# Three edits in a float32 network kernel: the up-projection's moving operand joined to 512 columns, the router's choice taken from logits, and slot weights as one product of six columns

## The reference

```python
def conv_glu_ffn(x, w_up, conv_w, conv_b, w_down):
    h = x @ w_up
    g, u = h[..., :D_FF], h[..., D_FF:]
    g = causal_depthwise_conv(g, conv_w, width=3) + conv_b
    return (jax.nn.silu(g) * u) @ w_down
```

```python
g_prob = softmax(h @ w_rg + b_rg)                  # 4 groups
g_top, g_idx = top_k(g_prob, 1)
e_in = (h @ w_re + b_re)[chosen group]             # 8 experts
e_top, e_idx = top_k(softmax(e_in), 2)
wts = g_top * e_top / sum(e_top)
y = sum over the two experts: wts * ((silu(h @ w_g[e]) * (h @ w_u[e])) @ w_d[e])
x = x + y
x = x + (p @ w_ple) * sigmoid(rmsnorm(x) @ w_ple_gate)
out = rmsnorm(x)
```

## Time and profile before

| | |
|---|---|
| Median of 3 executions | 1065.79 us (1063.05 to 1066.69) |
| The profiled execution's own time | 1061.78 us |
| Its span in the profile | 1060.0 us |
| PE busy | 1014.4 us (96%), weight loads 781.1 |
| DVE busy | 630.1 us (59%) |
| ACT busy | 533.6 us (50%) |
| POOL busy | 86.5 us (8%) |
| Bytes moved | 224.62 MB, mean 212 GB/s |

### The profile page before, as it was taken

How to read it: one execution, slowest core, us unless ns; L and a number is a source line. 1 busy time by engine, 2 the same in 40 slices (tenths; PEclk the granted TensorE clock), 3 DMA queues, 4 the chain that set the end, 5 groups by cost and what they waited for, 6 DMA issues and landing times.

```text
span 1060.0 us, 15388 instructions
## 1 busy us (share of the span) xinstructions
PE 1014.4 (96%) x6023; PEld 781.1 (74%) x6023; DVE 630.1 (59%) x1242; ACT 533.6 (50%) x941; POOL 86.5 (8%) x98
## 2 busy tenths in 40 slices
PE   7999899999999999999999999997989999999977
PEld 6777599999888876799999888775655455545445
DVE  4778678888646576678888547668642121212156
ACT  6667565555436566665555447746522122112255
POOL 0100002112000211002112002100000000000000
PEclk9999999999999999999999999999999999999999
DMA  8824255664565533465654563155459999999931
GB/s 279 312 89 150 81 159 163 196 199 160 200 197 178 180 127 113 125 193 161 198 199 160 186 187 129 41 165 196 162 174 410 409 409 409 409 409 409 405 110 40
DMA packets 112672, 224.62 MB, mean 212 GB/s; under 512 B 10559, under 2 KB 65234, under 8 KB 112594
## 3 DMA queue, kind: packets, MB, share of 16 engines
q1 hardware_dynamic: 112434, 223.04, 60.0%
q10 hardware_dynamic: 160, 0.53, 0.1%
HBM read 222.50 MB, written 1.05 MB: 211 GB/s over the span
## 4 chain that ended last, share of the span: by engine, by line
PE 86%; DVE 8%; ACT 3%; issue 1%; SPq 1%; DMA 1%; DVEq 0%; ACTq 0%
PE ps L543 82%; PE ps L547 4%; DVE wl L1890 1%; DVE smb L1904 1%; SPq L2795 1%; DMA ring<-in_w_in_even_dram 1%; DVE xs L1890 1%; DVE pb L1895 0%; ACT hh L1354 0%; DVE smb L1890 0%; ACT wh L1357 0%; ACT xh L1357 0%; SPq L2792 0%; DVE hl L1900 0%; ACT xg L1354 0%
## 5 line engine op out<-in xcount | busy, mean ns | idle before, releaser
L1890 DVE TENSOR_TENSOR wl<-ring,wh 128x1024 fp32r<-128x1024 f32 (+3 forms) x212 | 278.4, 1322 | 132.3 <-ACT wh L1357 130.9
L1357 ACT ACTIVATE wh<-ring 128x1024 fp32r<-128x1024 f32 (+3 forms) x212 | 222.6, 1052 | 147.1 <-PE ps L543 142.7
L543 PE MATMUL ps<-hh,wh 128*128 128x256 f32 x768 | 218.9, 286 | 1.4 <-DVE sA L1890 1.0
L543 PE MATMUL ps<-hh,wl 128*128 128x256 f32 x768 | 216.8, 283 | 0.0
L543 PE MATMUL ps<-hl,wh 128*128 128x256 f32 x768 | 215.1, 283 | 0.0
L543 PEld LDWEIGHTS ps<-hh,wh 128*128 128x128 f32 x768 | 147.6, 192 | 3.2 <-DVE wl L1890 1.4
L543 PEld LDWEIGHTS ps<-hh,wl 128*128 128x128 f32 x768 | 147.5, 192 | 0.0
L543 PEld LDWEIGHTS ps<-hl,wh 128*128 128x128 f32 x768 | 146.5, 192 | 0.3
L543 PE MATMUL ps<-ring,xg 128*64 128x512 f32 x320 | 85.5, 595 | 0.0
L2743 POOL TENSOR_TENSOR fs<-fs,rt 128x256 f32<-128x256 f32 x44 | 52.5, 1212 | 364.5 <-ACT fs L1354 364.5
L543 PE MATMUL ps<-wh,hh 128*128 128x512 f32 (+3 forms) x192 | 79.7, 415 | 2.1 <-DVE wl L1890 2.0
(11 more groups left out here) (287 smaller groups left out, 1679.7 us busy)
## 6 DMA issues: line engine op xcount, KB each, us to landing
ring<-in_w_up_dram SPq DMA_DIRECT2D x88, 512.0 KB, 4.7
ring<-in_w_down_dram SPq DMA_DIRECT2D x22, 1024.0 KB, 5.0
ring<-in_w_gate_e_dram SPq DMA_DIRECT2D x40, 512.0 KB, 7.8
ring<-in_w_up_e_dram SPq DMA_DIRECT2D x40, 512.0 KB, 9.5
ringx<-in_w_down_e_dram SPq DMA_DIRECT2D x16, 1024.0 KB, 8.7
ring<-in_w_down_e_dram SPq DMA_DIRECT2D x16, 1024.0 KB, 9.9
ring<-in_w_in_odd_dram SPq DMA_DIRECT2D x12, 1024.0 KB, 5.1
ringx<-in_w_gate_e_dram SPq DMA_DIRECT2D x24, 512.0 KB, 10.0
```

Of the source, the lines that this page charges most:

```text
L543: return e.matmul(o, l, r, start=start, stop=stop)
L1357: return e.activation(o, i, ACT.Copy)
L1890: return e.tensor_tensor(o, a, b, op)
```

## The change

Three parts; the names of a part's pieces are in brackets.

1. Up-projection (`gemm_up`). The high and low parts of the activation lie side by side in `hx`, so that one product of 512 columns with `wh` gives high by high in a bank's columns 0 to 255 and low by high in 256 to 511; `wl` by the high part stays a product of 256 columns. Only the first chunk of a layer keeps three products. Both halves have to be added: ACT copies the upper half to `low`, DVE adds it to the lower. So `conv` gets four ACT copies and two more DVE operations, `ups` (c = 1) is new, and `gate` multiplies out of SBUF.
2. Router. Group and experts are chosen on the logits with DVE's MAX and MAX_INDEX; the softmaxes move behind the first gathers. The reciprocal root, the splits of x and `select` are cut in halves and moved, the fourth `ple` product stands behind the ranks, and `slot_rows(0)` lies inside `gate_up(0)`.
3. Slot weights. `w6` holds the three columns' high and low parts in `F32R`; one product of six columns replaces the float32 one of three, ACT copies 12 columns to `wt6` and DVE adds. `slot_rows(g)` for later g stands behind the gather of odd i.

```diff
+        r1, hxf, ffh, ffl, ft, gq, low = opened(("hx", [P, 8, 2, S], F32R), *FF)
+        hhf, hlf = hxf[:, :, 0, :], hxf[:, :, 1, :]
...
+            def gemm_up(name, norm, c0, banks4, after, fresh):
+                for c in range(4):
+                    wh_, wl_ = weights(c0 + c, wh, wl, 2)
...
+                            if fresh and c == 0:
+                                mm(b[:, 0:S], wh_[:, kc, ms], hhf[:, k, :], k == 0, False)
+                            else:
+                                mm(b[:, :].rearrange("p (a s) -> p a s", a=2), wh_[:, kc, ms], hxf[:, k, :, :], k == 0, False)
+                            w = mm(b[:, 0:S], wl_[:, kc, ms], hhf[:, k, :], False, k == 7)
...
# ACT, ffn
                 def conv(s):
+                    for m in range(4):
+                        b = filled(q, ("ff", l, s), m)
+                        if s and m % 2 == 0:
+                            emptied(q, ("ff", l, s - 1), m + 1)
+                        copy(low[:, m, :], b[:, S:2 * S]).then_inc(s_low, 1)
                     for m in range(2):
-                        emptied(q, ("ff", l, s), m)
+                        q.wait_ge(s_gq, 2 * (11 * l + s) + m + 1)
...
# DVE, ffn
-                        w = tt(gq[:, m, :], b[:, 0:S], rb, ALU.mult)
+                        tt(gq[:, m, :], b[:, 0:S], low[:, m, :], ALU.add).then_inc(of(drained, ("ff", l, s), m), 1)
+                    for m in range(2):
+                        emptied(q, ("ff", l, s), m)
+                        tt(gq[:, m, :], gq[:, m, :], rb, ALU.mult).then_inc(s_gq, 1)
...
+                def ups(s):
+                    for m in range(2):
+                        b = filled(q, ("ff", l, s), 2 + m)
+                        q.wait_ge(s_low, 4 * (11 * l + s) + m + 3)
+                        tt(ft[:, m, :], b[:, 0:S], low[:, 2 + m, :], ALU.add).then_inc(of(drained, ("ff", l, s), 2 + m), 1)
...
-                        tt(ft[:, m, :], b[:, 0:S], fs[:, m, :], ALU.mult).then_inc(of(drained, ("ff", l, s), 2 + m), 1)
+                        tt(ft[:, m, :], ft[:, m, :], fs[:, m, :], ALU.mult).then_inc(s_ft, 1)
...
# PE, router and experts
+            for t, n in ((0, 0), (0, 1), (1, 0)):
+                embed(t, n)
             q.wait_ge(s_msk, 1)
...
+            embed(1, 1)
...
-                        w = mm(b2[:, 3 * j:3 * j + 3], slots_of(i, t).bitcast(F32), w3[:, t, i, :], t == 0, t == 1)
+                        w = mm(b2[:, 6 * j:6 * j + 6], slots_of(i, t), w6[:, t, i, :], t == 0, t == 1)
...
+                    if i == 0 and k == 4:
+                        slot_rows(0)
...
+                if i < 14 and i % 2:
+                    slot_rows(i // 2 + 1)
                 act_T(i)
...
# DVE, router
+            own.inc(red(mt, lgr, ALU.max))
+            own.inc(tt(goh, lgr, bc(mt, 4), ALU.is_equal))
...
+                w = e.max(m8[:, t, :], ing[:, t, :])
...
+                w = e.max_index(i8[:, t, :], m8[:, t, :], ing[:, t, :])
...
             tt(msk, oh1, oh2, ALU.add).then_inc(s_msk, 1)
+            x_lo(1, 0)
...
+            select(0, 0)
+            x_lo(1, 1)
```

More of the change, by code:

```diff
@@ L1210, in tensor, with embed @@
             up = unit_in(q, u_ple).rearrange("p (k n) -> p k n", k=2)
[L1211 to L1217, removed]
+            def embed(t, n):
+                b = claim(2 * t + n, "ple", t, n)
+                for k in range(2):
+                    w = mm(b[:, :], ppT[:, k, t * P:(t + 1) * P], up[:, k, n * 512:(n + 1) * 512], k == 0, k == 1)
+                w.then_inc(of(full, "ple", t, n), 1)
+            for t, n in ((0, 0), (0, 1), (1, 0)):
+                embed(t, n)
             q.wait_ge(s_msk, 1)
@@ L1224, in tensor @@
             mm(b[:, 64:96], cst[:, C_ONE:C_ONE + P], msk[:, 1, :], False, True).then_inc(of(full, "rank"), 1)
+            embed(1, 1)
+            unit_done[u_ple] = (of(full, "ple", 1, 1), use["ple", 1, 1][1] + 1)
             def gather(g, part):
-                if part == 0 and g % 2 == 0:
-                    q.wait_ge(s_sel, g // 2 + 1)
+                if part == 0:
+                    q.wait_ge(s_sel, g + 1)
                 for m in range(2 * part, 2 * part + 2):
@@ L1777, in scalar @@
             warm()
+            for n in range(2):
+                emptied(q, (2, "out"), 0, n)
+                copy(xhk[:, 0, 64 * n:64 * n + 64], xk[:, 0, 64 * n:64 * n + 64]).then_inc(s_xhi, 1)
             q.wait_ge(s_cl, CLATE)
@@ L1808, in slot_rows @@
                 b = filled(q, "wsl", g)
[L1809 to L1814, removed]
+                if g >= 2:
+                    q.wait_ge(s_wsl, g - 1)
+                copy(wt6[:, g % 2, :, :].rearrange("p j c -> p (j c)"), b[:, 0:12]).then_inc(of(drained, "wsl", g), 1)
             def gate_hi(c):
@@ L1964, in norm_T @@
                                 st[:, 1:2]))
[L1965 removed]
+                if name not in ("nm2", "nf2"):
                     q.wait_ge(s_sq, SQ[name])
@@ L2285, in ffn @@
                         split_lo(c0 + 4 * s + c + 3, wh, wl)
-                        if s and c != 1:
-                            (conv, None, gate, split)[c](s - 1)
+                        if s:
+                            (conv, ups, gate, split)[c](s - 1)
                 for j in range(17):
@@ L2616, in gather @@
                 w.then_inc(of(drained, "xg", g, m), 1)
-            select(0)
+            select(0, 0)
+            x_lo(1, 1)
+            own.inc(red(m5, rl5, ALU.max))
+            tt(pr5, rl5, m5.unsqueeze(3).to_broadcast([P, 2, 5, 8]), ALU.subtract).then_inc(s_smi, 1)
+            gather(0, 0)
             b = filled(q, "rank")
@@ L2652, in vector @@
                 if i % 4 == 1 and i < 12:
-                    select(i // 4 + 1)
+                    for h in range(2):
+                        select(i // 4 + 1, h)
                 if i < 14:
                     gather(i // 2 + 1, i % 2)
+                if i < 14 and i % 2:
+                    slot_rows(i // 2 + 1)
                 for n in range(2):
```

193 lines of the change are left out of this document (116 added, 77 removed).

## The result

The changed kernel takes **1045.67 us** (median of 4 runs, 1042.79 to 1046.11), the kernel before beside it 1064.66. The ratio is 0.983, 95% interval 0.980 to 0.986: faster by 19.0 us. The two profiled executions differ by 1061.8 - 1045.7 = 16.1 us, and since only these can be taken apart, the account is made with them.

What follows compares the result with a forecast made beforehand. PE, busy for 96% of the span, was taken as the bound. Terms 8.4 + 5.2 + 3.1 = 16.7 us took the profiled 1061.8 to 1045.1, and 4.0 more for the median gave 1049 us; range 1043 to 1059.

Steps and rivals of the forecast that it cites:

- Up-projection, PE: Up-projection: joining two 256-column products into one of 512 saves 0.0122 us, 688 times, 8.4 us; a block becomes 11.13 us.
- The cover: Up-projection: DVE keeps up with its added work, needing 10.9 to 11.1 us of a block's 11.13.
- POOL's relief: Up-projection on DVE: ups parts the two splits beside POOL's products, so about half of their 1.07 us loss, 0.5, goes.
- 0.41 at most: Up-projection on DVE: price of each new product by rb out of SBUF, 0.41 us at most, against 0.35 out of PSUM.
- By a hair: Up-projection: PE stays the bound by a hair, DVE needing 10.9 to 11.1 us of a block's 11.13.
- DVE rival: Up-projection: DVE becomes the bound of a block, 11.4 to 11.6 us as before; nothing gained there, 1057 us; chance 17%.
- Router: Router through gate_up(0): earlier mask, PE's queue last, gather starting at 769.2 instead of 772.64; net 5.2 us (3.5 to 6.5).
- Slot weights: Expert loop: eight instructions of 0.11 us become four, 7 rounds x 0.44 = 3.1 us; DMA's reserve hides its falling back.

Runs made afterwards that it cites:

- three_products: The changed kernel with the joined product of 512 columns issued as two of 256 again, ACT's and DVE's new work kept: 1054.49 us, ratio 0.993.
- slack1: The changed kernel with one more 128x256 float32 operation that nobody reads on DVE in each block, ahead of conv: 1051.25 us, ratio 0.990.
- slack2: The changed kernel with two more 128x256 float32 operations that nobody reads on DVE in each block, ahead of conv: 1053.62 us, ratio 0.993.
- tail_fill: The changed kernel with nine products of 512 columns filling PE's pause right behind the last scatter: 1044.03 us, ratio 0.981.
- joining_alone: The kernel before with the up-projection's part of the change alone, router and slot weights as before: 1052.58 us, ratio 0.991.
- ups_moved: The changed kernel with ups moved behind the third split, so the two splits beside POOL's products are adjacent again: 1048.63 us, ratio 0.987.

## Why the prediction was right

Foretold were 1049 us and 16.7 us gained. Against the profiled execution's own time 1045.1 us were foretold and 1045.7 came. The median is 3.3 us lower than foretold, because I carried over the 4.0 us by which before's median lay above its profile; the changed kernel's median is its profile's time. Those 4.0 us were an accident of three runs: in the experiments before's medians are 1061.8 to 1063.3, at most 1.5 above that profile. Before's runs lie from 1059.5 us at a mean granted clock of 0.993 to 1067.2 at 0.983, the changed kernel's four at 0.992 to 0.995. Whether the clock falls less often in the changed kernel isn't settled: three_products, slack1 and slack2, with the new router too, have runs at 0.987. There is luck in the sum as well: of parts that had no term in it, the tail lost 1.2 us and the untouched parts won 0.9.

- **Up-projection, PE**: right. A pair is 11.095 / 32 = 0.3467 us. The 768 columns of a pair at 2.4 GHz are 0.320, so a product has 0.0133 us beside its columns; three products of 256 give (0.360 - 0.320) / 3, the same. 8.9 us came instead of 8.4: 8.9 / 688 = 0.0129 us saved each time and not 0.0122. My 0.228 for 512 columns was 1 ns too high, since I divided a piece that ends with a product's whole duration; the starts are 0.2267 apart. By the gap of the Trainium skill (TensorE: Matmul & The Clock Gate, Back-to-back issue gap) 1.7 us would have been won, an estimate; the trace doesn't agree.
- **The cover**: right, with 0.1 us more room than foretold: 10.78 us with the wait for the bias, of a block of 11.10, where I had 10.9 to 11.1. In the parts: 1.34 us for both new pairs, the bottom of my range, and POOL's relief 0.51 to 0.56. The row that I had called "0.41 at most" for SBUF pairs measured 0.335, as out of PSUM. The Trainium skill (VectorE: DVE Perf Modes, The TRN2 errata) gives 424 ns for such an operation by its (N + 151) / 0.96, an estimate. Here one of a pair starts 0.335 us behind the other, and a pair lasts 0.75: as a duration the trace agrees, as a price in a sum it is 27% too high.
- **"By a hair"**: the bound was right and its consequence mis-sized. I priced a shortfall of DVE at the shortfall. slack1 shows a step: with DVE's 11.12 us against PE's 11.09, one wait early in the layer, and then 0.22 us a block through PE's pace; slack2 shows that the pace can come back at a later wait. My DVE rival's chance was the right worry; its mechanism was incomplete.
- **Router**: mask 9.8 us behind the transposes (10.9 foretold), gather 15.4 (15.5), at the full clock as foretold, `gate_up(0)` without a wait. 5.0 us of 5.2. What I didn't see is that in each run the clock falls in the embedding products or not. The row from which I took 6.5 us for twelve of them was at the lower level itself:

```profile
759.70:762.00 2.30, 2.30 (x4) 1.10 (x4) 2.12 (x3) 2.26 (x3) 0.00 (x0) 0.50 0.00 0
```

The changed kernel's profile fell in the same way, so that my term met is partly luck: with the clock at 1.00, as in tail_fill, the router is another 1.7 us shorter, a gain that the order before couldn't take. In joining_alone the sixteen embedding products ran at 1.00 and PE then waited 2.44 us for the mask.

- **Slot weights**: the loop gave 2.5 us of 3.1. The products are 0.42 us a pair (0.44 foretold), plus 0.2 by the new place, which I hadn't priced, less 1.7 us in all for a wait that I hadn't looked for: I counted DVE's operations as lying beside `scatter` and didn't ask which bank PE takes next behind `slot_rows`. DMA fell back as foretold: still 409 GB/s, and the landing of the earlier trace rows grew from 11.9 to 13.4 us there and to 14.6 between 940 and 975 us, where before still has 11.8. PE never waits for it.

```profile
ringx<-in_w_up_e_dram SPq DMA_DIRECT2D x1, 512.0 KB, 13.4
```

- **Tail**: 1.2 us lost to the lottery of the clock, in no term of mine.

## What to carry to other kernels

Price a product as its columns plus a fixed part, read both from the distances of starts at two widths in the same trace, and join products that share stationary weights where an engine with room can add the halves. Before an instruction is moved past another, look which bank or buffer its engine takes next and who has to empty it. Where two engines run neck and neck, test the reserve by adding known work in small steps: the price need not be proportional.

## What I had not expected of the hardware

The stream of 512 and 256 columns has two paces at a granted clock of 1.00, 11.09 and 11.31 us a block. A single wait of 0.24 us sets the slower one for the remaining 93 us of the up-projection (slack1 and ups_moved, both layers), and in slack2, with a wait in each block, it comes and goes. What a product has beside its columns is 13.3 ns at the one pace and 16.7 at the other: (0.3534 - 0.320) / 2.

The granted clock falls to its lower level in the router's embedding products, which PE issues without a gap (6 of 12 profiles), and in pauses of 2.3 us (6 of 11), and not always: 1.7 and 1.3 us that come and go between executions of one design.

A split on DVE (both operands in SBUF) takes 1.77 us beside POOL's products and 1.21 elsewhere; a pair of additions out of PSUM beside them keeps its 0.67 us.
